# Recurrent rounds in quarter tiles: transposes and all projection steps by 64x64 tiles, the next pair's first inverse at the fifth level, bias rows copied in the first feed-forward stage

## The reference

```python
def step(state, inp):                       # RWKV-7, per head of 64, over 512 tokens
    r_t, w_t, k_t, v_t, a_t, b_t = inp
    sa = jnp.einsum('bhij,bhj->bhi', state, a_t)
    state = (state * w_t[:, :, None, :] + sa[..., None] * b_t[:, :, None, :]
             + v_t[..., None] * k_t[:, :, None, :])
    return state, jnp.einsum('bhij,bhj->bhi', state, r_t)
var = jnp.mean(jnp.square(y - mean), axis=-1, keepdims=True)   # per head, then normed, gated, @ w_o
x = x + swiglu_ffn(rms_norm(x, ffn_norm[layer]), ffn_w_in[layer], ffn_w_out[layer])
bias = band_bias(rel_bias[:, g * 16:(g + 1) * 16], window, dilation)   # attention, per head
```

## Time and profile before

| what | us |
|---|---|
| median of 3 runs (lowest, highest) | 1780.49 (1779.56, 1787.06) |
| the profiled execution | 1777.27 |
| span of its instructions | 1775.5 |
| PE busy, in 15388 records | 1742.2 |
| DVE busy | 904.0 |
| ACT busy | 742.5 |
| POOL busy | 202.0 |

### The profile page before, as it was taken

The page is one execution under the profiler, slowest core; times in us unless marked ns, Lnnn a source line. Parts: engine busy times, 40 slices in busy tenths (PEclk is TensorE's granted clock), DMA queues, the critical chain, the costliest instruction groups (busy, mean ns, idle before and its releaser), DMA issues.

```text
span 1775.5 us, 35844 instructions
## 1 busy us (share of the span) xinstructions
PE 1742.2 (98%) x15388; PEld 1351.5 (76%) x15388; DVE 904.0 (51%) x1567; ACT 742.5 (42%) x1285; POOL 202.0 (11%) x172
## 2 busy tenths in 40 slices
PE   7999999999999999999999999999999999999999
PEld 2746666666478888888888888888887788888887
DVE  6825555554454444333556656655656544444321
ACT  6434444432243222222565665565655532222211
POOL 0033344431100000000111111111110000000000
PEclk9999999999999999999999999999999999999999
DMA  4321222231133223333322222322222233333332
GB/s 128 99 64 61 88 68 68 66 104 62 60 96 95 95 95 96 106 95 95 104 81 89 84 83 73 85 82 83 84 84 72 72 95 95 95 98 101 98 95 95
DMA packets 58453, 155.00 MB, mean 87 GB/s; under 512 B 6503, under 2 KB 23447, under 8 KB 58296
## 3 DMA queue, kind: packets, MB, share of 16 engines
q1 hardware_dynamic: 58200, 152.63, 27.7%
q10 hardware_dynamic: 96, 0.07, 0.0%
HBM read 150.51 MB, written 11.61 MB: 91 GB/s over the span
## 4 chain that ended last, share of the span: by engine, by line
PE 92%; DVE 4%; ACT 2%; issue 1%; DMA 1%; POOL 1%; SPq 0%; ACTq 0%; DVEq 0%; POOLq 0%
PE bank L618 89%; PE bank L621 2%; DVE f L2278 1%; DVE f L2193 0%; DVE r L2107 0%; ACT f L1684 0%; ACT r L1369 0%; DMA f<-xT 0%; ACT f L1686 0%; DMA f<-stream 0%; DMA f<-const 0%; DVE r L1785 0%; DVE f L1796 0%; DVE f L1809 0%; DVE f L1837 0%
## 5 line engine op out<-in xcount | busy, mean ns | idle before, releaser
L618 PE MATMUL bank<-r 128*128 128x512 f32 x5424 | 1253.4, 391 | 2.4 <-DVE r L2107 1.0
L618 PEld LDWEIGHTS bank<-r 128*128 128x128 f32 x5424 | 1012.6, 188 | 221.2 <-issue 6.2
L618 PE MATMUL bank<-f 64*64 64x64 f32 (+6 forms) x9532 | 457.1, 279 | 24.8 <-issue 5.2
L1785 DVE TENSOR_TENSOR r<-f,r 128x1024 fp32r<-128x1024 f32 x222 | 283.9, 1279 | 362.6 <-ACT r L1369 362.3
L618 PEld LDWEIGHTS bank<-f 64*64 64x64 f32 (+3 forms) x9532 | 291.3, 138 | 183.7 <-issue 112.3
L1369 ACT ACTIVATE r<-f 128x1024 fp32r<-128x1024 f32 x222 | 232.4, 1048 | 146.3 <-PE bank L618 141.5
L2465 POOL TENSOR_TENSOR r<-f,r 128x512 fp32r<-128x512 f32 x48 | 66.9, 1394 | 807.6 <-ACT r L1673 807.6
L1652 ACT ACTIVATE r<-f 128x512 fp32r<-128x512 f32 x44 | 27.8, 632 | 215.6 <-DVE f L2146 215.6
L2176 DVE TENSOR_TENSOR f<-bank,f 128x512 f32<-128x512 f32 x72 | 56.1, 778 | 74.9 <-PE bank L618 72.2
L1684 ACT ACTIVATE f<-bank,f 128x512 f32<-128x512 f32 x48 | 33.0, 688 | 101.5 <-PE bank L618 100.8
L1649 ACT ACTIVATE f<-f 128x512 f32<-128x512 f32 x44 | 27.8, 632 | 110.5 <-DVE f L2136 110.5
(11 more groups left out here) (117 smaller groups left out, 926.2 us busy)
## 6 DMA issues: line engine op xcount, KB each, us to landing
f<-stream SPq DMA_DIRECT2D x246, 512.0 KB, 3.6
bias_copies<-bias_rows SPq DMA_DIRECT2D x6, 1536.0 KB
f<-xT SPq DMA_DIRECT2D x16, 256.0 KB, 4.4
f<-lora_out SPq DMA_DIRECT2D x16, 128.0 KB, 6.2
f<-bias_copies SPq DMA_DIRECT2D x64, 32.0 KB, 2.4
f<-bias_copies SPq DMA_DIRECT2D x32, 64.0 KB, 2.1
outT<-f SPq DMA_DIRECT2D x8, 256.0 KB, 4.5
f<-const SPq DMA_DIRECT2D x1, 576.0 KB, 3.7
```

Of the source, the lines that this page charges most:

```text
L618: return nc.tensor.matmul(out, lhsT, rhs, start=start, stop=stop, skip_group_check=True)
L1785: TT(r(lo_at(q), 1024), f(O_RAW + panel_of(q) % RAW * 1024, 1024), rf(hi_at(q), 1024), ALU.subtract).then_inc(s["w_lo"], 1)
```

## The change

- All 16 projection steps of a pair's round are done in quarters (`quartered` no longer looks at the step).
- The four transposes are made of 64x64 products against the identity or the centring matrix, head 0 into bank 0 and head 1 into bank 1 (`flip_corners`); the two banks become one PSUM tensor, `sides`, so that ACT reads both at once. Removals and b are transposed together and share one signal. The four uses take turns in the list of bank 0.
- The sum for the variance moves from bank 0 to bank 7, behind a new signal `var_ln`.
- `first_inverse(k + 1)` moves from behind `solve` to between `off_diagonal(k, 5)` and `next_inverse(k, 5)`; `b_scores(k + 1)` to right behind `solve(k)`; `k_scores(k + 1)` one step later. DVE's order follows, and its `partial(3)` moves behind the masks of the b scores.
- `copy_bias` becomes 48 transfers of 192 KB, one behind each panel from the seventh of the first feed-forward stage on.

The diff:

```diff
--- before.py
+++ after.py
@@ -254,3 +254,5 @@
         ctx.enter_context(nc.sbuf_tensor("whole_map", [P, TOTAL], F32))
-        banks = [ctx.enter_context(nc.psum_tensor(f"bank{i}", [P, 512], F32)) for i in range(8)]
+        sides = ctx.enter_context(nc.psum_tensor("sides", [P, 1024], F32))
+        banks = [sides[:, 0:512], sides[:, 512:1024]]
+        banks += [ctx.enter_context(nc.psum_tensor(f"bank{i}", [P, 512], F32)) for i in range(2, 8)]
         bias_rows = nc.dram_tensor("bias_rows", [3 * 16 * 384], F32, kind="Internal").ap()
@@ -350,3 +352,2 @@
-        QUARTERED = (0, 3, 4, 6, 7, 9, 10, 11, 12, 13, 14, 15)
         NEAR, FAR = banks[6], banks[3]
@@ -355,3 +356,3 @@
         def quartered(k, step):
-            return 0 <= k < NHP and step in QUARTERED
+            return 0 <= k < NHP
@@ -399,6 +400,5 @@
-        SIDE = {0: [("b_tr", 0), ("akv", 0), ("bonus", 1), ("var", -1),
+        SIDE = {0: [("v_tr", 0), ("b_tr", 0), ("akv", 0), ("k_tr", 0), ("bonus", 1),
                     ("first", 1), ("bsc", 1), ("ksc", 1), ("w", 2), ("g", -1)],
-                1: [("kk", 1), ("v_tr", 0), ("a_tr", 0), ("k_tr", 0), ("first", 1), ("bsc", 1), ("ksc", 1),
-                    ("a", 2)]}
+                1: [("kk", 1), ("first", 1), ("bsc", 1), ("ksc", 1), ("a", 2)]}
         SIDE_TURN = {b: {use: n for n, use in enumerate(each_iteration(SIDE[b]))} for b in SIDE}
@@ -546,6 +546,7 @@
-                lo = n * 8 * 384
-                copies = bias_copies[lo * P:(lo + 8 * 384) * P]
-                sp.dma_start(copies.rearrange("(h i u) -> h i u", h=8, i=P),
-                             bass.AP(tensor=bias_rows.tensor, offset=lo, ap=[[384, 8], [0, P], [1, 384]]))\
+                if n == 0:
+                    sp.wait_ge(s["bias_dma"], 48)
+                copies = bias_copies[n * P * 384:(n + 1) * P * 384]
+                sp.dma_start(copies.rearrange("(i u) -> i u", i=P),
+                             bass.AP(tensor=bias_rows.tensor, offset=n * 384, ap=[[0, P], [1, 384]]))\
                     .then_inc(s["bias_rep"], 16)
@@ -566,6 +567,2 @@
                     x_back(1)
-                if 0 <= k < 6:
-                    if k == 0:
-                        sp.wait_ge(s["bias_dma"], 48)
-                    copy_bias(k)
                 if k == NHP - 2:
@@ -587,2 +584,4 @@
                     sp.dma_start(f(O_WHI + LAST_AT, 1024), wo_last).then_inc(s["wo_last"], 16)
+                if 0 <= p - PAN_IN0 - 6 < 3 * 16:
+                    copy_bias(p - PAN_IN0 - 6)
                 hp, i = divmod(p - PAN_QKV, 9)
@@ -591,3 +590,3 @@
                     if hp == 0 and h == 0:
-                        sp.wait_ge(s["bias_rep"], 96)
+                        sp.wait_ge(s["bias_rep"], 16 * 3 * 16)
                         sp.wait_ge(s["hd_lo"], FC)
@@ -738,2 +737,3 @@
                     pe.wait_ge(s["y_sb"], NHP)
+                    pe.wait_ge(s["var_ln"], NHP)
                 elif first:
@@ -812,3 +812,3 @@
             def variance_ready(hp):
-                fill(0, "var", hp)
+                pe.wait_ge(s["y_sb"], hp + 1)
                 pe.wait_ge(s["y_sq"], hp + 1)
@@ -826,30 +826,32 @@
+            def flip_corners(at, off, by):
+                for q in range(NT):
+                    for e in range(2):
+                        for h in range(2):
+                            last = mm(banks[h][CH * e:CH * (e + 1), at + q * HD:at + (q + 1) * HD],
+                                      half(off(q) + e * CH, h), half(O_CON + by + h * HD, h))
+                return last
             def value_flip(hp):
-                fill(1, "v_tr", hp)
+                fill(0, "v_tr", hp)
+                if hp + 1 < NHP:
+                    side_read(pe, 1, "kk", hp + 1)
+                else:
+                    side_read(pe, 1, "ksc", hp)
                 if hp:
                     projection_kept(pe, proj_of_value(hp))
-                for q in range(NT):
-                    last = mm(banks[1][:, q * P:(q + 1) * P], f(vin(hp) + q * P, P), con(C_CENTRE))
-                last.then_inc(s["v_tr"], 1)
-            def removal_flip(hp):
-                fill(1, "a_tr", hp)
-                pe.wait_ge(s["ar_a"], hp + 1)
-                for q in range(NT):
-                    last = flip(banks[1][:, q * P:(q + 1) * P], f(chunk(O_AR, hp, 2 * P, q, 0), P))
-                last.then_inc(s["a_tr"], 1)
+                flip_corners(0, lambda q: vin(hp) + q * P, C_CENTRE).then_inc(s["v_tr"], 1)
-            def b_flip(hp):
+            def removal_and_b_flip(hp):
                 fill(0, "b_tr", hp)
+                pe.wait_ge(s["ar_a"], hp + 1)
+                flip_corners(0, lambda q: chunk(O_AR, hp, 2 * P, q, 0), C_ID)
                 pe.wait_ge(s["bt"], hp + 1)
-                for q in range(NT):
-                    last = flip(banks[0][:, q * P:(q + 1) * P], f(chunk(O_BT, hp, P, q, 0), P))
-                last.then_inc(s["b_tr"], 1)
+                flip_corners(4 * HD, lambda q: chunk(O_BT, hp, P, q, 0), C_ID).then_inc(s["b_tr"], 1)
             def k_flip(hp):
-                fill(1, "k_tr", hp)
+                fill(0, "k_tr", hp)
                 pe.wait_ge(s["kt"], hp + 1)
-                for q in range(NT):
-                    last = flip(banks[1][:, q * P:(q + 1) * P], f(chunk(O_KT, hp, P, q, 0), P))
-                last.then_inc(s["k_tr"], 1)
+                flip_corners(0, lambda q: chunk(O_KT, hp, P, q, 0), C_ID).then_inc(s["k_tr"], 1)
@@ -859,2 +861,4 @@
                     fill(h, "first", hp)
+                if hp:
+                    side_read(pe, 0, "k_tr", hp - 1)
                 pe.wait_ge(s["ar_a"], hp + 1)
@@ -917,3 +921,3 @@
                 side_read(pe, 1, "ksc", hp)
-                side_read(pe, 1, "v_tr", hp)
+                side_read(pe, 0, "v_tr", hp)
@@ -985,3 +989,3 @@
                 side_read(pe, 0, "b_tr", hp)
-                side_read(pe, 1, "k_tr", hp)
+                side_read(pe, 0, "k_tr", hp)
                 for h in range(2):
@@ -1031,2 +1035,3 @@
                         pe.wait_ge(s["y_sb"], hp)
+                        pe.wait_ge(s["var_ln"], hp)
                 else:
@@ -1078,4 +1083,3 @@
                 if here:
-                    removal_flip(k)
-                    b_flip(k)
+                    removal_and_b_flip(k)
                     next_inverse(k, 2)
@@ -1111,26 +1115,43 @@
                 if here:
-                    off_diagonal(k, 5, (lambda q, h: sum_beside(0, O_Y, "var_ps", q, h)) if before else None)
+                    off_diagonal(k, 5, (lambda q, h: sum_beside(7, O_Y, "var_ps", q, h)) if before else None)
                 elif before:
-                    head_sum(0, O_Y, "var_ps")
-                project(k, 8)
-                if here:
+                    head_sum(7, O_Y, "var_ps")
+                if here and after:
+                    first_inverse(k + 1)
                     next_inverse(k, 5)
-                    project(k, 9)
+                    project(k, 8)
                     solve(k)
-                if after:
-                    first_inverse(k + 1)
-                if not here:
+                    b_scores(k + 1)
                     project(k, 9)
-                project(k, 10)
-                if here:
                     transitions(k)
-                project(k, 11)
-                if after:
-                    b_scores(k + 1)
-                project(k, 12)
-                if here:
+                    project(k, 10)
+                    project(k, 11)
                     readout(k)
-                if after:
+                    project(k, 12)
                     k_scores(k + 1)
-                project(k, 13)
+                    project(k, 13)
+                elif here:
+                    project(k, 8)
+                    next_inverse(k, 5)
+                    project(k, 9)
+                    solve(k)
+                    project(k, 10)
+                    transitions(k)
+                    project(k, 11)
+                    project(k, 12)
+                    readout(k)
+                    project(k, 13)
+                else:
+                    project(k, 8)
+                    if after:
+                        first_inverse(k + 1)
+                    project(k, 9)
+                    project(k, 10)
+                    project(k, 11)
+                    if after:
+                        b_scores(k + 1)
+                    project(k, 12)
+                    if after:
+                        k_scores(k + 1)
+                    project(k, 13)
                 project(k, 14)
@@ -1503,14 +1524,22 @@
+            def flipped(at):
+                return sides[:, :].rearrange("p (h q n) -> p h q n", h=2, n=HD)[:, :, at * NT:(at + 1) * NT, :]
+            def tokens(off):
+                return bc(f(off), (HD, 2), (P, NT), (1, HD))
             def keep_value(hp):
-                side(1, (s["v_tr"], hp + 1), f(O_VTOK))
```

(25 more changed lines are left out.)

10 lines of the change are left out of this document (5 added, 5 removed).

## The result

The changed kernel takes **1788.72 us** (median of 12 runs, 1785.57 to 1791.92); the kernel before, beside it, 1780.24 (12 runs, 1777.58 to 1787.06). The ratio is 1.004, 95% interval 1.0029 to 1.005: slower by 0.3 to 0.5%. I had forecast 1769.8 with a range up to 1781.

What follows compares the result with a forecast made beforehand. TensorE, busy 98%, was taken as the bound, with gaps from instruction-block fetches. Terms -6.8 - 1.2 + 0.7 - 3.0 - 0.4 = -10.7 us from 1777.27 gave 1766.6; 3.2 for the runs' median made 1769.8, range 1762 to 1781.

Steps and rivals of the forecast that it cites:

- instruction blocks: TensorE's waits for 256-instruction blocks in the recurrence: four rounds' gaps give 2.5 us, against 5.5 before; -3.0 us.
- Value transpose and step 1: From the small products' end through projection step 1: 1.33 us instead of 2.21, 0.85 gained in 8 rounds; -6.8 us.
- rival 3: New transposes run at the pace of two quadrants, 27 ns a record: +2.1 us, 1782.6; chance 0.03.
- Removal and b transposes: These transposes and projection step 2: 0.2 us gained, 0.15 counted because ACT's copies start later, times 8; -1.2 us.
- key transpose: Key transpose and projection step 5: 1.33 us instead of 1.58, but level 4 can't start earlier; 0.
- early projection: Early output projection: added waits for DVE's additions, against a 1.6 us TensorE wait now behind the readout; -0.4 us.
- rival 1: Steps bound by hand-overs: transpose savings return as waits for the inverse's copy; -2.7 us, 1777.8; chance 0.24.
- Level 5 order: Reordered steps around level 5, with the readout waiting for the states: about +0.1 us in seven rounds; +0.7 us.
- Bias copies: Smaller copies in the feed-forward stage, hidden because panels are issued more than a panel ahead; 0.
- issue gaps over 5 us: Sign of failure: TensorE gaps without a semaphore wait adding up to over 5 us would prove the forecast wrong.
- Rival 2: Crowded instruction blocks decide: 13.2 us at 3.55 us spacing, 1780.5; at 3.75, 1793; chance 0.14.

Runs made afterwards that it cites:

- level5_only: The kernel before with only the new order around level 5 and the variance's sum in bank 7; 1787.61 us, ratio 1.0042.
- flips_only: The changed kernel with the order around level 5 put back as before; 1795.88 us, ratio 1.0087 to the kernel before.
- copies_only: The kernel before with only the bias copies moved to the first feed-forward stage; 1778.31 us, ratio 0.9986.
- value_step1: The kernel before with only the value transpose and projection step 1 in quarters, shared banks, variance sum in bank 7 and moved copies; 1779.3 us, ratio 0.9992.
- probe1024: The kernel before with 1024 extra 64x64 products, without semaphores, ahead of the recurrence; 1837.54 us in one run.

## Why the prediction was wrong
The step that failed is the term **instruction blocks, -3.0 us**. It measured **+16.7** (gaps 22.2 for 5.5). Everything else came out right as a sum: I had -7.7 for the other terms, and the rest went from 336.5 to 329.0, -7.5. That it agrees to 0.2 us is partly luck: the rest is good to about 2 us, and of its parts, by the experiments, the first gave 4.3 for my 6.8 and the others 2.7 for my 0.9. The two together are the 9.2 us by which the recurrence is longer (351.2 for 342.0).

Four things were wrong inside that term.
- *The laying of the cuts.* I counted three short blocks in each of four rounds, with shortfalls of 0.1 to 0.3 us. There are 36 gaps of 0.6 us on average. I let each dense block keep the lead of the one before it; the gaps behind prompt requests, which follow blocks of 3.1 to 4.8 us, are 13.9 us for before's 4.5.
- *The request.* I took a request right behind the cut for granted. In the changed kernel some 8 of the gaps, 8.3 us of the sum, follow a request more than 1.7 us behind the cut (before: 1.0). What holds a request back isn't settled: it comes at the same place of the program in every round of the same phase, with and without transfers beside it.
- *The base.* I took before's 5.5 us as its density. It is a phase: 12.0 and 13.9 us when shifted. About 5 of the 16.7 us are the loss of this phase (mean of the three phases 10.5), and about 14 are what the change adds at any phase (mean of its three 24.7), less some 2.5 by which it is better than the mean of its phases. Of the 14, by the same means, some 6 lie behind prompt requests and some 8 behind late ones. The first are the density of the blocks. For the second no run shows a cause; that level5_only has nearly nothing else speaks for the new order, flips_only with 4.7 against the number of instructions. With one trace a phase these shares are rough.
- *The copies.* Their removal was to relieve the blocks. copies_only shows that it doesn't.

The other steps, in the order of the prediction:
- *Value transpose and step 1, -6.8.* The window in which this stands:
```profile
220.19:221.47 1.28, 1.28 (x47) 0.76 (x44) 1.27 (x3) 1.15 (x3) 0.00 (x0) 1.00 0.05 13
```
  1.28 us, where I had 1.33, for 2.21 before. The transposes run at 14.7 ns a record over four quadrants (32 records in 0.47 us, from 220.14), so rival 3 is out. Locally the step is right; over the recurrence value_step1 shows only 4.3 of the 6.8 (rest 331.7 against copies_only's 336.0), with the 2 us of uncertainty of such a difference.
- *Removal and b transposes, key transpose, early projection, -1.6 together.* Only their sum shows: from value_step1 to the change the rest falls by 2.7, with the order at level 5 in it, for my -0.9. No wait for the kept inverse appears among the waits after; rival 1 is out. The 1.6 us wait of the earlier trace rows for DVE's far-bank addition in `partial` (L2008) is down to 0.3 (L2038 after), nearly as forecast.
- *Level 5 order, +0.7.* The readout waits 0.20 us in all 8 rounds, the size that the earlier trace rows had:
```profile
289.90 2.67 PE L617 MATMUL bank<-f 64*64 64x64 f32 x104 [0.20 <-DVE f L1981]
```
  Alone it raised the rest by 2.0, no more than the uncertainty. Missing in the step was what the order is for: without it step 8 in quarters waits 10.0 us for `add_far`. I had looked for such waits only with the order already in.
- *Bias copies, 0.* Right within 0.2%.

What I named as a sign of failure, issue gaps over 5 us, came at 16.7, and the two rounds above last 41.8 and 40.6 us where I had 39.5. **Rival 2**, to which I gave 0.14, is the nearest: crowded blocks that no lead carries. For them it had 13.2 us at a spacing of 3.55, and the gaps behind prompt requests are 13.9. At that spacing it gave 1780.5. What is missing up to the measured 1788.7 is the size of the 8.3 us behind late requests, which stood in none of the rivals. Blocks that end in a gap after a prompt request took 3.78 us in the median here (3.54 before). The spacing is no constant: probe1024 has three values between 3.45 and 4.00 for equal blocks. I had used a value near the low end as if it were the price. The Trainium skill's page "Runtime: NRT & Kernel Launch", section "Instruction fetch mechanics", holds that crossing a block is mostly hidden. In 100 us of the feed-forward stage, where TensorE is busy throughout, these traces agree. In the recurrence they don't: 11 of some 68 crossings cost 5.5 us before, 36 of some 76 cost 22.2 in the changed kernel.

## What to carry to other kernels
Splitting a product into quadrants saves array time and pays in instructions: a step in quarters gives 0.2 us and costs 12 instructions, a quartered pair of transposes (removals and b) 112. Where 256 instructions are worked off in under some 4 us, the slowest spacing of probe1024, count instructions as you count microseconds, and take the idle time without a semaphore from the trace before you add any. And before a small change is judged, shift the cuts by a few dozen harmless instructions in both kernels: here the phase alone was worth 3 to 5 us, about half of what separates the two kernels. Then take more than one trace of each.
